# Strassen's seven products in nine of sixteen row tiles of each MLP's second product

## The reference, cut to what matters

```python
D_MODEL = 1024; SEQ = 256; DEPTH = 2; D_FF = 4 * D_MODEL
def _mlp(x, norm_g, w1, w2):
    h = _rmsnorm(x, norm_g)
    return jnp.square(jax.nn.relu(h @ w1)) @ w2
# for layer in range(DEPTH):  x = x + mixer(x);  x = x + _mlp(x, ...)
```

## Time and profile before

| | |
|---|---|
| median of 3 runs | 974.27 us (974.17 to 974.36) |
| span of the profiled execution, first to last instruction | 973.0 us |
| between the two | 1.3 us |
| PE busy | 964.8 us |
| DVE busy | 701.5 us |
| ACT busy | 551.6 us |
| mean granted TensorE clock | 0.999 |

### The profile page before, as it was taken

One profiled execution on the slowest core, in us unless ns is written; L12 is line 12 of the kernel. 1 busy time (PEld: TensorE's weight loads), 2 busy tenths in 40 slices (PEclk: granted clock), 3 DMA queues, 4 the chain that ended last, 5 costly groups with the idle time before them and its releaser, 6 DMA issues.

```text
span 973.0 us, 14065 instructions
## 1 busy us (share of the span) xinstructions
PE 964.8 (99%) x5352; PEld 825.9 (85%) x5352; DVE 701.5 (72%) x1085; ACT 551.6 (57%) x949; POOL 154.1 (16%) x189
## 2 busy tenths in 40 slices
PE   9999999999999999999999999999999999999997
PEld 8878888888888888888888888888888888988885
DVE  6888676766666757786667656666758989778884
ACT  6688665444555554455456444554535857766662
POOL 2741018920001102220001000000550110000000
PEclk9999999999999999999999999999999999999999
DMA  9985545565554664345555665555544463643631
GB/s 340 297 225 192 181 130 183 194 222 181 173 195 154 216 214 131 130 134 212 173 173 179 202 209 189 173 186 179 208 153 153 151 196 111 193 132 130 216 131 43
DMA packets 110339, 174.73 MB, mean 180 GB/s; under 512 B 4289, under 2 KB 73025, under 8 KB 110273
## 3 DMA queue, kind: packets, MB, share of 16 engines
q1 hardware_dynamic: 109840, 173.40, 54.3%
q10 hardware_dynamic: 432, 0.44, 0.1%
HBM read 172.78 MB, written 1.05 MB: 179 GB/s over the span
## 4 chain that ended last, share of the span: by engine, by line
PE 92%; DVE 3%; POOL 1%; issue 1%; DMA 1%; SPq 1%; ACT 0%; POOLq 0%; DVEq 0%
PE ps L552 24%; PE ps L505 19%; PE ps L503 11%; PE ps L445 9%; PE ps L447 9%; PE ps L446 9%; PE ps L502 3%; PE ps L521 2%; PE ps L680 1%; PE ps L660 1%; PE ps L519 1%; PE ps L648 1%; DMA xs<-in_x 1%; PE ps L604 1%; DVE wlo L1536 1%
## 5 line engine op out<-in xcount | busy, mean ns | idle before, releaser
L1536 DVE TENSOR_TENSOR wlo<-raw,whi 128x1024 fp32r<-128x1024 f32 x312 | 373.3, 1235 | 16.4 <-PE ps L552 8.3
L1027 ACT ACTIVATE whi<-raw 128x1024 fp32r<-128x1024 f32 x312 | 315.5, 1048 | 35.6 <-PE ps L552 21.8
L505 PE MATMUL ps<-hT,whi 128*128 128x512 f32 x784 | 279.5, 396 | 0.0
L503 PE MATMUL ps<-hT,wlo 128*128 128x256 f32 x896 | 231.7, 279 | 0.0
L552 PE MATMUL ps<-whi,ur 128*128 128x512 f32 x656 | 181.6, 389 | 0.0
L503 PEld LDWEIGHTS ps<-hT,wlo 128*128 128x128 f32 x896 | 168.9, 188 | 9.1
L505 PEld LDWEIGHTS ps<-hT,whi 128*128 128x128 f32 x784 | 147.1, 188 | 30.3
L552 PEld LDWEIGHTS ps<-whi,ur 128*128 128x128 f32 x656 | 123.0, 188 | 24.4
L445 PE MATMUL ps<-whi,hT 128*128 128x512 f32 (+1 forms) x312 | 122.1, 391 | 0.0
L447 PE MATMUL ps<-whi,hT 128*128 128x512 f32 (+1 forms) x312 | 120.0, 385 | 0.0
L446 PE MATMUL ps<-wlo,hT 128*128 128x512 f32 (+1 forms) x312 | 119.9, 384 | 0.0
(11 more groups left out here) (233 smaller groups left out, 1310.6 us busy)
## 6 DMA issues: line engine op xcount, KB each, us to landing
raw<-in_w SPq DMA_DIRECT2D x64, 1024.0 KB, 5.6
raw<-in_w_in SPq DMA_DIRECT2D x34, 1024.0 KB, 5.1
raw<-in_w_in_o SPq DMA_DIRECT2D x24, 1024.0 KB, 5.2
raw<-in_w_out_o SPq DMA_DIRECT2D x8, 1024.0 KB, 4.9
raw<-in_w_in_e SPq DMA_DIRECT2D x5, 1024.0 KB, 13.1
raw<-in_w_mem SPq DMA_DIRECT2D x4, 1024.0 KB, 12.1
raw<-in_w_out_e SPq DMA_DIRECT2D x4, 1024.0 KB, 5.1
raw<-in_w_out SPq DMA_DIRECT2D x4, 1024.0 KB, 4.9
```

The source lines that it names most:

```text
L503: mm = e.matmul(o[:, 0:256], l[:, k, :], hT[0][:, k, :], start=False, stop=False)
L505: mm = e.matmul(o, h[:, k, :], both, start=False, stop=k == 7)
L1027: e.activation(split_half(i)[0], raw_half(i), ACT.Copy).then_inc(*up("hi", ("hi", i)))
L1536: e.tensor_tensor(l, raw_half(i), h.bitcast(F32), ALU.subtract).then_inc(*up("lo", ("lo", i)))
```

## The change

Tiles 1, 2, 4, 5, 7, 8, 10, 11 and 13 of each w2 take seven products of blocks in place of eight, after Strassen. Such a tile has four parts (`"s"`, high and low of each): the first block column as loaded, one block as loaded, then two pairs of blocks that DVE has summed in place in the raw buffer (`weights_added`, four sums of 128 x 512). DVE also makes three sums of u blocks (`u_sums`), and u has up to eight slots. The sums go into seven banks; the seven-product tiles share four of them (`b1`, `b5`, `b6`, `b7`), which `sums_shared` folds into the residual with nine DVE operations once tile 13 is done. The ordinary tiles (0, 3, 6, 9, 12) add into banks 2, 0, b5 and 3 with a difference of u blocks (`four`); tiles 14 and 15 are as before. With seven banks held, one is left for the first product: both of its blocks share it, and each is three matmuls of 256 columns (`t_half`, and `w1_first` for tile 0, which has two banks). ACT takes relu out of that bank and squares it (`relu_squared`); DVE's adding and its square are gone. The lookahead orders of ACT and DVE in the MLP are written anew. Helpers that turned a half's number into a tile's (`i // 2`) use a table (`tile_of`, `last_half`); SQ2 moves and has eight slots. `up` and `at` get three new semaphores.

```diff
+SEVEN = (1, 2, 4, 5, 7, 8, 10, 11, 13)
...
+    if by == "s":
+        return (r[:, :, 0:512], r[:, 1:2, 512:1024], r[:, :, 512:1024], r[:, :, 0:512])[x]
...
+def ur1(p):
+    return tuple(t[:, 0:4, :].rearrange("p (k b) n -> p k (b n)", b=2) for t in us[p % 2])
+def slots(p):
+    return (1, 8) if p in SEVEN else (0, 4) if p >= 14 else (0, 6)
...
+    def block3(stage, n, a, b, opened, stop=False):
+        name = ("acc", stage, n)
+        if name not in opened:
+            take(*name)
+        mm = mm3(bank(*name), a, b, name not in opened, stop)
+        opened.add(name)
+        return mm
+    def seven(stage, layer, p, opened, last):
+        i, (uh, ul) = first_half["w2", layer, p], us[p % 2]
+        a21, a11, a22, a12, e3, e1, t2, e4 = ((uh[:, k, :], ul[:, k, :]) for k in range(8))
+        for x, products in enumerate((((0, a11, "b1"), (1, a12, 2)), ((0, e4, 3),), ((0, e1, "b5"), (1, e3, "b7")),
+                                      ((0, t2, "b6"), (1, a22, 0)))):
+            h, l = weights(i + x)
+            for t, a, n in products:
+                mm = block3(stage, n, a, (h[:, t, :], l[:, t, :]), opened, last and n in ("b1", "b5", "b6", "b7"))
+            if x < 3 or not last:
+                mm.then_inc(*up("wd", ("wd", i + x)))
+            else:
+                mm.then_inc(*up("mm", ("accs", stage), ("wd", i + x)))
+        if last:
+            for n in ("b6", "b7", "b1", "b5"):
+                give("acc", stage, n)
+    def four(stage, layer, p, opened):
+        i, (uh, ul) = first_half["w2", layer, p], us[p % 2]
+        for x in range(2):
+            h, l = weights(i + x)
+            a2, a1, d = ((uh[:, k, :], ul[:, k, :]) for k in (2 * x, 2 * x + 1, 4 + x))
+            for a, c, n in ((a1, 0, 2), (a2, 0, 0), (a2, 1, "b5"), (d, 1, 3)):
+                mm = block3(stage, n, a, tuple(y[:, 0, 512 * c:512 * c + 512] for y in (h, l)), opened)
+            mm.then_inc(*up("wd", ("wd", i + x)))
...
+    def w1_first(label, stage, between):
+        b = [take("mm", label, m)[:, 0:256] for m in range(2)]
+        for half in range(2):
+            for m in range(2):
+                h, l = weights(first_half[label] + m)
+                for k in range(4 * half, 4 * half + 4):
+                    w.wait_ge(*at(*x_split(stage, k)))
+                    mm = mm3(b[m], (h[:, k, :], l[:, k, :]), (hT[0][:, k, :], hT[1][:, k, :]), k == 0, k == 7)
+                if half:
+                    mm.then_inc(*up("mm", ("mm", label, m), ("wd", first_half[label] + m)))
+                    give("mm", label, m)
+                elif m == 0:
+                    between()
-        t_first(("w1", layer, 0), f"mlp{layer}", lambda: x_transposed(f"mlp{layer}", before, 1))
-        for j in range(17):
-            if j == 1:
-                t_pair(("w1", layer, j), f"mlp{layer}")
+        stage, opened = f"mlp{layer}", set()
+        w1_first(("w1", layer, 0), stage, lambda: x_transposed(stage, before, 1))
+        for j in range(1, 17):
+            if j < 16:
+                for m in range(2):
+                    t_half(("w1", layer, j), m, 256, 8, hT, lambda k: x_split(stage, k))
+            p = j - 1
+            w.wait_ge(*at("ul", layer, p))
+            if p == 15:
+                acc_last_by_columns(stage, ("w2", layer, p), ur1(p), 0,
+                                    lambda: x_transposed(("ret", "sec")[layer], stage, 0))
+            elif p == 14:
+                take("acc", stage, 1)
+                for x in range(2):
+                    acc_half(stage, ("w2", layer, p), x, ur1(p), 0, fresh=() if x else (1,))
+            elif p in SEVEN:
+                seven(stage, layer, p, opened, p == SEVEN[-1])
+            else:
+                four(stage, layer, p, opened)
...
+            if tiles[tile_of[i]][6] == "s" and part_of(i) >= 2:
+                w.wait_ge(*at("q", i))
...
         for j in range(17):
             if j < 16:
                 used(("w1", layer, j), 1)
-                rl, sq, u, d = RL[j % 2], SQ2[j % 2], ur[(j // 2) % 2], 2 * (j % 2)
-                if j >= 2:
-                    w.wait_ge(*at("sq2", layer, j - 2))
-                for m in range(2):
-                    low_copied(("w1", layer, j), m, rl[:, m * 256:m * 256 + 256])
-                w.wait_ge(*at("sq2", layer, j))
-                if j >= 4:
-                    w.wait_ge(*at("wd", first_half["w2", layer, 2 * (j // 2) - 3] + 1))
-                e.activation(u[0][:, d:d + 2, :], two(sq), ACT.Copy).then_inc(*up("xh", ("uh", layer, j)))
+                relu_squared(layer, j)
             if j >= 1:
-                used(("w2", layer, j - 1), 1)
+                i = first_half["w2", layer, j - 1]
+                weights_to(before_sums(i + 2 + HI_AHEAD, last_half[tile_of[i]] + LO_AHEAD))
+            if j < 16:
+                u_high(layer, j)
+            if j >= 1:
+                weights_to(last_half[tile_of[i]] + HI_AHEAD)
             if layer == 0:
                 decays(j)
+    def before_sums(n, lows):
+        for i in range(lows, n):
+            if tiles[tile_of[i]][6] == "s" and part_of(i) == 2:
+                return i
+        return n
+    def relu_squared(layer, j):
+        label, rl, sq = ("w1", layer, j), RL[j % 2], SQ2[j % 2]
+        if j >= 2:
+            w.wait_ge(*at("ul", layer, j - 2))
+        if j == 0:
+            for m in range(2):
+                w.wait_ge(*at("mm", label, m))
+                e.activation(rl[:, 256 * m:256 * m + 256], bank("mm", label, m)[:, 0:256], ACT.Relu).then_inc(
+                    *up("aev", ("rl", layer, j) if m else ("rl0", layer), ("free", ("mm", label, m))))
+        else:
+            w.wait_ge(*at("mm", label, 0))
+            e.activation(rl, bank("mm", label, 0), ACT.Relu).then_inc(*up("aev", ("rl", layer, j), ("free", ("mm", label, 0))))
+        w.wait_ge(*at("rl", layer, j))
+        e.activation(sq[:, 0:4, :], rl.rearrange("p (k n) -> p k n", k=4), ACT.Square).then_inc(*up("asq", ("sq2", layer, j)))
+    def u_high(layer, j):
+        k0, k1 = slots(j)
+        w.wait_ge(*at("sq2", layer, j) if j >= 14 else at("us", layer, j))
+        if j >= 2:
+            w.wait_ge(*at("wd", last_half[tile_of[first_half["w2", layer, j - 2]]]))
+        e.activation(us[j % 2][0][:, k0:k1, :], SQ2[j % 2][:, k0:k1, :], ACT.Copy).then_inc(*up("xh", ("uh", layer, j)))
...
+            if tiles[tile_of[i]][6] == "s" and part_of(i) == 1:
+                weights_added(i)
         done[0] = max(done[0], n)
+    def weights_added(i):
+        r = v3(raw[tile_of[i] % NRAW], 2)
+        b11, b12, b21, b22 = r[:, 0, 0:512], r[:, 0, 512:1024], r[:, 1, 0:512], r[:, 1, 512:1024]
+        w.wait_ge(*at("lo", i))
+        e.tensor_tensor(b22, b22, b12, ALU.add).then_inc(*up("qs", ("q3", i)))
+        w.wait_ge(*at("q3", i))
+        e.tensor_tensor(b12, b12, b11, ALU.add).then_inc(*up("qs", ("q", i + 1)))
+        w.wait_ge(*at("q", i + 1))
+        e.tensor_tensor(b11, b11, b22, ALU.add).then_inc(*up("qs", ("q2", i)))
+        w.wait_ge(*at("q2", i))
+        e.tensor_tensor(b21, b21, b11, ALU.add).then_inc(*up("qs", ("q", i + 2)))
+        w.wait_ge(*at("q", i + 2))
...
+                w.wait_ge(*at("f8", stage))
...
+    def u_sums(layer, j):
+        sq = SQ2[j % 2]
+        w.wait_ge(*at("sq2", layer, j))
+        if j in SEVEN:
+            e.tensor_tensor(sq[:, 4:6, :], bc(sq[:, 0:1, :], 128, 2, 128), sq[:, 1:3, :], ALU.subtract).then_inc(
+                *up("us", ("u3", layer, j)))
+            w.wait_ge(*at("u3", layer, j))
+            e.tensor_tensor(sq[:, 6, :], sq[:, 1, :], sq[:, 5, :], ALU.subtract).then_inc(*up("us", ("u2", layer, j)))
+            w.wait_ge(*at("u2", layer, j))
+            e.tensor_tensor(sq[:, 7, :], sq[:, 3, :], sq[:, 6, :], ALU.subtract).then_inc(*up("us", ("us", layer, j)))
+        else:
+            e.tensor_tensor(sq[:, 4:6, :], sq[:, 1:4:2, :], sq[:, 0:3:2, :], ALU.subtract).then_inc(*up("us", ("us", layer, j)))
+    def u_low(layer, j):
+        k0, k1 = slots(j)
+        w.wait_ge(*at("uh", layer, j))
+        hi, lo = us[j % 2]
+        e.tensor_tensor(lo[:, k0:k1, :], SQ2[j % 2][:, k0:k1, :], hi[:, k0:k1, :].bitcast(F32), ALU.subtract).then_inc(
+            *up("xl", ("ul", layer, j)))
+    def sums_shared(stage):
+        b1, b5, b6, b7 = (bank("acc", stage, n) for n in ("b1", "b5", "b6", "b7"))
+        ri = [stats(("i", stage, tb), 1) for tb in range(2)]
+        x0, x1, x2, x3_ = (xs[:, 512 * i:512 * i + 512] for i in range(4))
+        v, w_, y, z = (VW[:, i, :] for i in range(4))
+        w.wait_ge(*at("accs", stage))
+        e.tensor_copy(z, b6).then_inc(*up("fs", ("f0", stage), ("free", ("acc", stage, "b6"))))
+        w.wait_ge(*at("f0", stage))
+        e.tensor_tensor(v, b1, z, ALU.subtract).then_inc(*up("fs", ("f1", stage)))
+        w.wait_ge(*at("f1", stage))
+        e.tensor_tensor(w_, v, b7, ALU.subtract).then_inc(*up("fs", ("f2", stage), ("free", ("acc", stage, "b7"))))
```

(57 more changed lines are left out.)

55 lines of the change are left out of this document (23 added, 32 removed).

## The result

The changed kernel takes 987.38 us (987.17 to 987.97, 4 runs) against 974.26 (974.17 to 974.36, 4 runs): ratio 1.0131, 95% interval [1.0117, 1.0146], slower by 13.1 us. The forecast was slower by 6.4, at 980.7, range 968 to 988. The profiled span is 985.4 us against 973.0, 12.4 more. Ahead of the prediction I put 1.3 us around the span of the kernel before, the median less the profiled span. That mixed two executions: in every execution of either kernel that has both numbers on record, 1.7 to 1.9 us lie around the span. The profiled execution of the kernel before was some 0.5 us slower than its median, so the 0.7 us between 13.1 and 12.4 is spread between executions, and no part of the change.

What follows compares the result with a forecast made beforehand. PE instructions were taken to bound the MLPs, with slack on DVE and ACT. From 974.3 us, -12.2 (second product) + 4.8 (first product) + 6.9 (pairs) + 3.9 (tail) + 3.0 (MLP 0) = +6.4 gave 980.7 us, range 968 to 988.

Steps and rivals of the forecast that it cites:

- (d): The forecast itself: the changed kernel takes 976.3 to 985 us; chance 0.48.
- PE alone: Both MLPs: seven-product tiles save 12.2 us, 256-column first product costs 4.8 (0.15 a step); -7.4 us in all.
- The pair: Second of two successive seven-product steps: high B3 delays relu, so low A0' reaches PE late; 0.87 us each, +6.9 us.
- The tail: Each MLP's end: DVE's nine fold operations delay low halves and u's low half; PE waits 0.65 and 1.3 us, +3.9 total.
- MLP 1, the three together: PE alone, The pair and The tail taken for one MLP: -3.7 + 3.5 + 1.95 = +1.7 us.
- MLP 0 alone: POOL's decays slow DVE's low halves; half of some 5.7 us, rounded up, reaches PE: +3.0 us (0 to 6).
- my own signs of being wrong: No PE waits in the MLPs, waits in ordinary steps, or 256-column matmuls at another pitch than 0.12 us.
- Costed at nothing: PSUM's one bank for w1 (2.2 us of cover), raw-tile transfers and ACT table loads: no cost charged.
- (a): Rival: the cover holds, stalls under 5.4 us in all; 966.9 us with none, 970.8 with the tail alone; chance 0.22.
- (b): Rival: stalls equal what PE saves, 972.3 to 976.3 us, pairs at 0.6 us and a tail of 1; chance 0.13.
- (c): Rival: DVE becomes the bound, dependent starts 0.11 us, full POOL contention, tail 6: -7.4 + 11 + 6 + 4 = 988; chance 0.17.

Runs made afterwards that it cites:

- the first product alone: Changed kernel with no seven-product tiles, second product as before: 984.55 us; with one ACT high half fewer in each MLP's last step as well, 981.65 us.

## Why the prediction was right in direction and short in size

- **The number.** 987.38 us is inside the stated range, at its upper edge, and outside of the forecast's own band (d), 976.3 to 985: the loss is twice the 6.4 us that the sum gave.
- **What bounds the kernel, PE alone.** Right. A seven-product tile saves 5.44 - 4.79 = 0.65 us (forecast 0.68), the first product costs 0.16 to 0.17 (0.15), the ordinary second product 0.02 more, which I had not counted. That is -3.3 us an MLP where -3.7 stood. The choice of 0.15 rested on a reading that was the wrong way round: in the earlier trace rows the run at 0.119 us has hT as the stationary operand (17.14 us), and the run at 0.1205 has the weight halves (832.04), as the change does. The same operands stood at the costlier end; the change came at 5.75 / 48 = 0.1198.
- **The pair.** Right in mechanism and place. Relu, the last sum and low A0' start or end within 0.02 us of the forecast, and PE's A0' 0.12 us early. A pair costs 33.09 - 32.30 = 0.79 us (0.87), of which 0.71 is in the tile and the rest at the w1 tile behind it. Shown: it goes when ACT's one high half moves ahead of relu, and when the sums are made small.
- **The tail.** Right in size and in the two waits named: +1.84 us (1.95). "Nothing hides it" was wrong. It is 1.1 us shorter when ACT's index alone moves, and 0.37 of it is there in the first product alone (9.90 us), where nothing is folded; why is open.
- **MLP 1, the three together.** Forecast -3.7 + 3.5 + 1.95 = +1.7, measured -3.3 + 3.2 + 1.8 = +1.7. So near a sum is partly luck: PE's gain was 0.4 too large and the stalls were 0.4 too large.
- **MLP 0 alone, the term that was mis-sized.** +3.0 stood for what is +6.3 over MLP 1. I charged half of the delay that DVE had with slack. The delay carried on into step 7, an ordinary step, where a wait was one of my own signs of being wrong, and into step 8. Cutting POOL gave back 5.4 of the 6.3. Why so much more reaches PE is in part argued: the changed kernel has more operations with two SBUF inputs, and POOL's work itself takes longer (its last add ends at 213.9 us in place of 199.7).
- **What had no term.** "Costed at nothing" did not hold a step that I should have priced: the lookahead written anew. I followed ACT's order in the middle of an MLP and not in its last step, where the extra half waits for the last tile and has the next layer's transposes behind it. The stretches behind the MLPs are 3.2 us longer for it; the run without that half is 3.0 us faster and has them as before. Nor did I ask what the orders would give if changed by one, which is worth 8 us.
- **The gap of 6.7 us** is, then, 3.2 in MLP 0 and 3.2 behind the MLPs. The remaining 0.3 is within the spread between executions.
- **Rivals.** (a) and (b) did not come; (c) had the size (988) by another way: dependent starts stayed at 0.03 to 0.04 us, its terms for pairs (11) and tail (6) were too high against 6.3 and 3.7, its 4 for POOL too low, and the 3.2 behind the MLPs were not in it. Its number being near is no credit.

## What to carry to other kernels

Saved matmuls are worth their time only while the helpers' queues stay ahead, and these fail by order before they fail by total: at 85 to 88% busy over three steps DVE cost 0.8 us a pair or nothing, by one index in ACT's program. When a lookahead is changed by one, follow it at the ends of the loop too, and list what stands behind the extra item. Put dense VectorE work where GpSimd is quiet: the same contention was free with 4 us of slack in a period of 11 and cost 5.4 us without. And compare spans or medians with their like: the profile is one execution, and here it was 0.5 us off the median.

## What the runs showed of the hardware

A tile of 24 matmuls of 512 columns takes 5.44 us in the kernel before (0.2268 each) and 5.465 behind a first product in 256-column form, with no wait in the trace. The extra 0.02 us is in the first four starts of the tile (0.93 us against 0.91); from then on the pitch is the same. What causes it is open.

POOL's eight adds of 128 x 384 take 1.01 to 2.00 us each in the kernel before. The shortest starts at 197.26, and DVE's square, which starts 0.25 us behind it, takes 1.31 us in place of 0.69.
